# Ten weight slots of a 32-expert MoE stage, joined into one ring in the order of consumption

## The reference, cut to what matters

```
logits = hf @ w_router + b_router                    # 256 tokens, 32 experts
top_val, top_idx = lax.top_k(logits, 4)
gates = softmax(top_val)
for each expert e, on the tokens that chose it:
    gu = xb @ w_gate_up[e] + b_gate_up[e]            # (1024 x 2048): 8 MB
    gate = min(gu[:, :1024], 7);  up = clip(gu[:, 1024:], -7, 7)
    glu = gate * sigmoid(1.702 * gate)
    y = ((up + 1) * glu) @ w_down[e] + b_down[e]     # (1024 x 1024): 4 MB
    out[tokens] += gate_weight * y
x = x + gate2 * out;  return rms_norm(x, final_norm_g)
```

## Time and profile before

| | us |
|---|---|
| median of 3 runs | 1252.24 (1250.06 to 1254.26) |
| profiled execution | 1254.92 |
| its span, first to last instruction | 1253.1 |
| TensorE busy | 1140.6 (91%) |
| VectorE busy | 451.5 (36%) |
| data moved | 465.13 MB, mean 371 GB/s |
| instructions | 13746 |

### The profile page before, as it was taken

One profiled execution on the slowest core, in us unless ns is written; L12 is line 12 of the kernel. 1 busy time (PEld: TensorE's weight loads), 2 busy tenths in 40 slices (PEclk: granted clock), 3 DMA queues, 4 the chain that ended last, 5 costly groups with the idle time before them and its releaser, 6 DMA issues.

```text
span 1253.1 us, 13746 instructions
## 1 busy us (share of the span) xinstructions
PE 1140.6 (91%) x5333; PEld 521.6 (42%) x5333; DVE 451.5 (36%) x975; ACT 116.4 (9%) x217; POOL 11.8 (1%) x12
## 2 busy tenths in 40 slices
PE   3999999997999999999999999998989898999996
PEld 1588678864333333333232323232333333232322
DVE  3467236527613141432313141313233231313143
ACT  1111122611000000000000000000000000000000
POOL 0000000003000000000000000000000000000000
PEclk9999999998999999999999999999999999999999
DMA  9997941167659999999999999999999999999994
GB/s 341 366 370 303 391 163 68 67 248 292 269 212 429 428 427 429 428 429 428 428 428 429 429 427 428 427 430 429 427 428 427 430 429 427 428 427 430 428 428 190
DMA packets 49025, 465.13 MB, mean 371 GB/s; under 512 B 5466, under 2 KB 6220, under 8 KB 21100
## 3 DMA queue, kind: packets, MB, share of 16 engines
q1 hardware_dynamic: 45592, 461.11, 88.3%
q10 hardware_dynamic: 3412, 3.74, 1.0%
HBM read 463.79 MB, written 1.05 MB: 371 GB/s over the span
## 4 chain that ended last, share of the span: by engine, by line
PE 52%; DMA 40%; DVE 4%; SPq 2%; issue 1%; ACT 1%; DVEq 0%; ACTq 0%
DMA arena<-in_w_gate_up 40%; PE ps L806 12%; PE ps L824 11%; PE ps L566 8%; PE ps L833 5%; PE ps L689 2%; PE ps L712 2%; PE ps L661 2%; PE ps L788 1%; SPq L370 1%; PE ps L560 1%; PE ps L483 1%; PE ps L529 1%; PE ps L796 1%; PE ps L516 1%
## 5 line engine op out<-in xcount | busy, mean ns | idle before, releaser
L806 PE MATMUL ps<-arena 128*64 128x512 f32 x2048 | 455.2, 597 | 33.9 <-DMA arena<-in_w_gate_up 33.9
L806 PEld LDWEIGHTS ps<-arena 128*64 128x64 f32 x2048 | 141.4, 137 | 345.9 <-issue 273.2
L824 PE MATMUL ps<-arena 128*64 128x512 f32 x1024 | 226.0, 594 | 0.7 <-issue 0.7
L1431 DVE TENSOR_SCALAR arena<-ps 128x512 f32<-128x512 f32 x32 | 22.1, 691 | 380.2 <-PE ps L806 380.2
L824 PEld LDWEIGHTS ps<-arena 128*64 128x64 f32 x1024 | 72.1, 137 | 149.3 <-issue 146.0
L1470 DVE TENSOR_TENSOR arena<-ps,arena 64x512 f32<-64x512 f32 x64 | 44.1, 689 | 188.5 <-PE ps L824 188.1
L566 PE MATMUL ps<-arena 128*128 128x256 f32 x448 | 97.7, 380 | 0.0
L566 PEld LDWEIGHTS ps<-arena 128*128 128x128 f32 x448 | 85.1, 190 | 13.8 <-issue 2.6
L1070 ACT ACTIVATE arena<-arena 128x512 f32<-128x512 f32 x32 | 20.1, 630 | 607.3 <-DVE arena L1431 607.3
L788 PE MATMUL ps<-arena 128*128 128x128 f32 x512 | 63.1, 283 | 10.8 <-DVE arena L1485 10.8
L788 PEld LDWEIGHTS ps<-arena 128*128 128x128 f32 x512 | 60.1, 197 | 14.7 <-issue 14.7
(11 more groups left out here) (240 smaller groups left out, 629.5 us busy)
## 6 DMA issues: line engine op xcount, KB each, us to landing
arena<-in_w_gate_up SPq DMA_DIRECT2D x128, 2048.0 KB, 31.3
arena<-in_w_down SPq DMA_DIRECT2D x62, 2048.0 KB, 23.6
arena<-in_w_ada SPq DMA_DIRECT2D x12, 2048.0 KB, 17.1
arena<-in_w_in SPq DMA_DIRECT2D x10, 2048.0 KB, 16.5
arena<-in_w_mix_out SPq DMA_DIRECT2D x2, 2048.0 KB, 8.9
arena<-in_w_down SPq DMA_DIRECT2D x4, 1024.0 KB, 28.5
arena<-in_w_hy_out SPq DMA_DIRECT2D x1, 2048.0 KB, 15.0
arena<-in_w_attn_out SPq DMA_DIRECT2D x1, 2048.0 KB, 19.0
```

The lines of the kernel that those rows point to most:

```text
L806: last = mm(ps[64 * h:64 * h + 64, 4 + b, :], hTp[:, k, s * 64:(s + 1) * 64], w[:, o:o + 512], start=False, stop=(k == KD - 1))
L824: last = mm(ps[64 * h:64 * h + 64, 6, :], lhs, rows[c][:, qq * D + h * 512:qq * D + (h + 1) * 512], start=(q == 0), stop=(q == 7))
```

## The change

The ten areas become one list `slots`. Weight blocks are numbered in the order in which TensorE consumes them (`block_at`: ten of pair 0, then twelve to each pair), block n goes to slot n mod 10, and waits until block n-10 is consumed, with a single counter `consumed` that both gate_up and down count up. Since twelve blocks to a pair don't divide by ten, the slot of each block differs from pair to pair; pairs 1 to 14 are written out with constants on the SyncE and TensorE queues (`FIXED` = 15), and the loop begins at pair 15, with slots fixed as `last_slot`. The first fill goes in the ring's order, and the slot `dft` is filled between the first two of the front's areas.

```
-        gu_a = ring[:NJ]
-        gu_b = [span("dft", 0, 4096), span("ur", 4096, 4096), span("ur", 0, 4096), span("x", 0, 4096)]
-        dn_row = ring[NJ:NJ + NC]
-        last_row = [at("ring", 2048 * c, 2048) for c in range(4)]
+        in8, in9, hy, att, mix0, mix1 = (ring[where[b] % 6] for b in blocks[-6:])
+        slots = [in8, span("dft", 0, 4096), in9, hy, att, span("ur", 4096, 4096), mix0, mix1,
+                 span("ur", 0, 4096), span("x", 0, 4096)]
+        NS = len(slots)
+        A0, DB, B0, DA, PAIR = 0, NJ, NJ + NC, 2 * NJ + NC, 2 * (NJ + NC)
+        FIXED = E // 2 - 1
+        def block_at(p, i):
+            return PAIR * (p - 1) + NS + i if p else i
+        def place(p, i):
+            if isinstance(p, int):
+                n = block_at(p, i)
+                return slots[n % NS], s_slot[n % NS], 16 * (n // NS + 1)
+            k = last_slot[i]
+            per = last_slot.count(k)
+            before = last_slot[:i].count(k)
+            return slots[k], s_slot[k], p * (16 * per) + 16 * (uses_before[k] + before + 1 - FIXED * per)
+        def used(p, i):
+            return block_at(p, i) if isinstance(p, int) else p * PAIR + (NS - PAIR + i)
...
+            wait_used(blocks[-6])
+            gate_up(place(0, 0), 0, 0)
+            sp.wait_ge(S["s_ps"], 2 * HEADS)
+            gate_up(place(0, 1), 0, 1)
+            wait_used(blocks[-5])
+            gate_up(place(0, 2), 0, 2)
+            wait_used(blocks[-4])
+            gate_up(place(0, 3), 0, 3)
+            gate_up(place(0, 4), 1, 0)
+            sp.wait_ge(S["pj_sb"], KD)
+            gate_up(place(0, 5), 1, 1)
+            sp.dma_start(b_down[0:E, :], a["b_down"][0]).then_inc(S["bd_in"], 16)
+            wait_used(blocks[-2])
+            gate_up(place(0, 6), 1, 2)
+            wait_used(blocks[-1])
+            gate_up(place(0, 7), 1, 3)
             sp.wait_ge(S["mix_ps"], 4)
-            gate_up(gu_b[2], s_gub[2], 1, 2)
+            down(place(0, 8), 0, 0)
             sp.wait_ge(S["res_ps"], 1)
             sp.wait_ge(S["xs_rdy"], TT)
             sp.wait_ge(S["bc_sb"], 8)
-            gate_up(gu_b[3], s_gub[3], 1, 3)
+            down(place(0, 9), 0, 1)
 
             def pair_of(p, e_a, e_prev, e_b):
                 for j in range(NJ):
-                    sp.wait_ge(S["gu_used"], p * 8 + (j - 7))
-                    gate_up(gu_a[j], s_gua[j], e_a, j)
+                    sp.wait_ge(S["consumed"], used(p, A0 + j - NS + 1))
+                    gate_up(place(p, A0 + j), e_a, j)
                 for c in range(NC):
-                    sp.wait_ge(S["dn_used"], p * 4 + (c - 3))
-                    down(c, e_prev)
+                    sp.wait_ge(S["consumed"], used(p, DB + c - NS + 1) if isinstance(p, int) else used(p, DA + c - PAIR + 1))
+                    down(place(p, DB + c), e_prev, c)
                 for j in range(NJ):
-                    sp.wait_ge(S["gu_used"], p * 8 + (j - 3))
-                    gate_up(gu_b[j], s_gub[j], e_b, j)
+                    sp.wait_ge(S["consumed"], used(p, B0 + j - NS + 1))
+                    gate_up(place(p, B0 + j), e_b, j)
                 for c in range(NC):
-                    sp.wait_ge(S["dn_used"], p * 4 + (c - 1))
-                    down(c, e_a)
+                    sp.wait_ge(S["consumed"], used(p, DA + c - NS + 1) if isinstance(p, int) else used(p, DB + c + 1))
+                    down(place(p, DA + c), e_a, c)
...
-            pair_of(1, 2, 1, 3)
+            for p in range(1, FIXED):
+                pair_of(p, 2 * p, 2 * p - 1, 2 * p + 1)
             sp.wait_ge(S["tables"], 2)
-            with sp.Fori(2, n_pairs) as p:
+            with sp.Fori(FIXED, n_pairs) as p:
...
-            with pe.Fori(1, n_pairs) as p:
+            for p in range(1, FIXED):
+                pair_of(p)
+            pe.wait_ge(S["tables"], 2)
+            n_pairs = pe.value_load(table_i[0:1, 48:49], min_val=E // 2, max_val=ITEMS // 2)
+            with pe.Fori(FIXED, n_pairs) as p:
+                pair_of(p)
```

More of the change, by code:

```diff
@@ L142, in build @@
         NJ, NC = 4, 2
-        gu_a = ring[:NJ]
-        gu_b = [span("dft", 0, 4096), span("ur", 4096, 4096), span("ur", 0, 4096), span("x", 0, 4096)]
-        dn_row = ring[NJ:NJ + NC]
-        last_row = [at("ring", 2048 * c, 2048) for c in range(4)]
-        fgB = at("ring", 4096 * 2, D)
-        junk = at("ring", 4096 * 3, 2048)
         y = b_down = span("prm", 0, D)
@@ L265, in build @@
             x1T_dve x1T_act part_ps part_sb log_ps top_rdy top_exp m_rdy rank_ps cnt_ps cnt_sb ex_ps g_all gt_ps gt_sb tables h2_rdy
-            gu_used dn_used tr_done sc_done ga_done pt_done
+            consumed tr_done sc_done ga_done pt_done
             g_rdy sig_rdy act_rdy actT_rdy y_rdy ga_sb pt_sb sel_rdy wt_rdy mask_rdy
@@ L270, in build @@
         s_front = [sem(f"front_in{j}") for j in range(6)]
-        s_gua = [sem(f"gate_up_a_in{j}") for j in range(NJ)]
-        s_gub = [sem(f"gate_up_b_in{j}") for j in range(NJ)]
-        s_dn = [sem(f"down_in{c}") for c in range(NC)]
+        s_slot = [sem(f"slot_in{k}") for k in range(10)]
+        s_last = [sem(f"last_down_in{c}") for c in range(4)]
         pj_bank = (0, 1, 4, 5)
@@ L327, in build @@
         w_gu, w_dn = a["w_gate_up"], a["w_down"]
+        in8, in9, hy, att, mix0, mix1 = (ring[where[b] % 6] for b in blocks[-6:])
[6 more added lines that the diff above has]
+            return PAIR * (p - 1) + NS + i if p else i
+        last_slot = [block_at(FIXED, i) % NS for i in range(DA)] + [block_at(FIXED, DB + c) % NS for c in range(NC)]
+        uses_before = [sum(n % NS == k for n in range(block_at(FIXED, 0))) for k in range(NS)]
+        def place(p, i):
[8 more added lines that the diff above has]
+            return block_at(p, i) if isinstance(p, int) else p * PAIR + (NS - PAIR + i)
+        final_slot = [block_at(FIXED + 1, c) % NS for c in range(NC)]
+        last_row = [slots[final_slot[c // 2]][:, 2048 * (c % 2):2048 * (c % 2 + 1)] for c in range(4)]
+        fgB = slots[last_slot[0]][:, 0:D]
+        junk = slots[last_slot[1]][:, 0:2048]
         block = ctx.enter_context(nc.Block())
@@ L364, in _, with gate_up @@
                     sp.dma_start(dft, a["t_dft"].rearrange("(t p) f -> p t f", p=P)).then_inc(S["dft_in"], 16)
-            def gate_up(dst, landed, expert, j):
+            def gate_up(place_, expert, j):
+                dst, landed, _ = place_
                 src = w_gu[expert, j] if isinstance(expert, int) else w_gu[bass.ds(expert, 1), j]\
@@ L370, in gate_up, with down @@
                 sp.dma_start(dst, src).then_inc(landed, 16)
-            def down(c, expert):
+            def down(place_, expert, c):
+                dst, landed, _ = place_
                 src = w_dn[expert, c] if isinstance(expert, int) else w_dn[bass.ds(expert, 1), c]\
                     .rearrange("o p n -> p (o n)")
[L375 to L390, removed]
+                sp.dma_start(dst, src).then_inc(landed, 16)
+            wait_used(blocks[-6])
[14 more added lines that the diff above has]
+            gate_up(place(0, 7), 1, 3)
             sp.wait_ge(S["mix_ps"], 4)
-            gate_up(gu_b[2], s_gub[2], 1, 2)
+            down(place(0, 8), 0, 0)
             sp.wait_ge(S["res_ps"], 1)
@@ L422, in _ @@
             e_b = expert_of(q * 2 + 1)
-            sp.wait_ge(S["gu_used"], q * 8 + 4)
+            sp.wait_ge(S["consumed"], used(q, A0 + NJ))
             for c in range(4):
                 sp.dma_start(last_row[c], w_dn[bass.ds(e_b, 1), c // 2, :, 2048 * (c % 2):2048 * (c % 2 + 1)]
-                             .rearrange("o p n -> p (o n)")).then_inc(s_gua[c], 16)
+                             .rearrange("o p n -> p (o n)")).then_inc(s_last[c], 16)
             sp.dma_start(fgB, a["final_norm_g"][:].partition_broadcast(P)).then_inc(S["fg_in"], 16)
@@ L797, in gate_up @@
                            sel_bias[E * b:E * b + E, h * 512:(h + 1) * 512], start=True, stop=False)
+                first = (B0 if s else A0) if not isinstance(p, int) or p else NJ * s
                 for j in range(NJ):
-                    w, landed = (gu_b[j], s_gub[j]) if s else (gu_a[j], s_gua[j])
-                    pe.wait_ge(landed, p * 16 + 16)
+                    w, landed, count = place(p, first + j)
+                    pe.wait_ge(landed, count)
                     for kk in range(2):
@@ L807, in gate_up @@
                                           w[:, o:o + 512], start=False, stop=(k == KD - 1))
-                    last.then_inc(S["gu_used"], 1)
+                    last.then_inc(S["consumed"], 1)
             def act_transpose():
@@ L813, in act_transpose, with down @@
                 last.then_inc(S["tr_done"], 1)
[L815 to L819, removed]
+            def down(pieces):
+                n = KD // len(pieces)
+                for c, (rows, landed, count) in enumerate(pieces):
+                    pe.wait_ge(landed, count)
                     for qq in range(n):
@@ L824, in down @@
```

(42 more changed lines are left out.)

## The result

| | before | changed |
|---|---|---|
| median, us | 1252.01 (1250.06 to 1254.26, 4 runs) | 1243.28 (1242.55 to 1244.15, 4 runs) |
| ratio to before | | 0.993 (0.9911 to 0.9949) |
| profiled execution, us | 1254.92 | 1242.55 |
| its span, us | 1253.1 | 1240.7 |

The change made the kernel 8.7 us faster (0.7%); 10.8 were forecast. Between the two profiled spans lie 12.4 us, 3.7 more than between the medians.

A forecast was written before the change was run, and what follows sets the result against it. Weight transfers were taken as the bound (58.75 us a pair, TensorE 55.0). An earlier block 14 (-13.8 us) and code fetches (+3.0) sum to -10.8 us: profiled 1244.1, median 1241.4, range 1237 to 1251.

The forecast's parts named there:

- The bound and the place: Transfers bound the kernel once stocked blocks are used; the one costly standstill is 345 to 359 us, before pair 1's first down.
- Part 1: Block waits in the ring: block 14 leaves at 344.9 instead of 358.67, gaining 13.8 us at every later landing.
- gap at block 20: Pair 1's tight place, margin about 1 us: no gap taken; a missed one would cost at most about 2.9 us.
- Part 2: The first fill of ten blocks in a new order, dft's moved to near 220 us: cost and gain 0.
- Part 3: TensorE's code written out for fourteen pairs: 28 more code packets beside the full weight queue, costing 3 us.
- near the even end: Choice of 3 us for code fetches, between 1.9 us spread evenly over 16 engines and 31 us on one.
- The 1.1 us over the first four fetches: Block 14's issue to pair 15's B3 landing: 854.8 us due, 855.9 taken; the four fetches within it cost 1.1 us together.
- Part 4: SyncE, VectorE and the end: SyncE's code under 0.1 us each way, work behind the last gate_up landing unchanged at 38.5 us.
- One engine for all code: Rival: all code fetches pass one transfer engine, costing 31 us against 13.8 gained, so +17, 1269 us; chance 8%.
- The fetches cost as in the first pair: Rival: 28 fetches at 0.55 us each cost 15 us, giving 1254; at half, 7.7 us, giving 1246; chance 12%.
- Free: Rival: code fetches cost the transfers nothing, the full 13.8 us stays, 1238.4 us; chance 15%.
- The idle time comes back: Rival: gaps before block 20 or several, 2.9 us each: 1244.3 us with one, 1247 with two; chance 10%.

The follow-up runs named there:

- e2: The changed kernel with one more SyncE wait ahead of block 14, until nine of the first ten blocks are consumed: 1256.63 us, ratio 1.0033 to the kernel before.
- e3: The changed kernel with FIXED = 2, only pair 1 in the ring, fixed slots and a six-block wait from pair 2: 1248.56 us, ratio 0.9969 to before.
- e6: The changed kernel with FIXED = 3, pairs 1 and 2 in the ring, the loop from pair 3: 1246.27 us, ratio 0.9956 to before.
- e9: The changed kernel with the first fill's dft transfer put back some 40 us later: 1243.32 us, ratio 0.9933 to before.
- e1: The kernel before, slots and waits kept, with pairs 1 to 14 written out on TensorE and SyncE: 1257.77 us, ratio 1.0043 to before.
- e8: The kernel before with pairs 1 to 14 written out on SyncE alone, TensorE keeping its loop: 1252.15 us, ratio 1.0004 to before.
- e5: The changed kernel with FIXED = 5, pairs 1 to 4 written out in the ring, the loop from pair 5: 1241.01 us, ratio 0.9907 to before.

## Why the prediction was right, point by point

**The bound and the place.** Right. Removing one stretch of idle transfers moved every later landing; putting back the wait in it (e2) took the gain away.

**Part 1.** Right in size: 13.8 us forecast, 12.9 to 13.4 us came back in e2. No gap at block 20, as forecast, with the interval of 28.8 us computed to 0.1. One sentence there was too short. It said that running up to ten blocks ahead "brings nothing". In the steady state that is so, but early on it is what keeps the 13.8 us, as e3 and e6 show for pairs 2 and 3. The calculation had assumed the ring there; it hadn't said that its depth does the work.

**Part 2.** Right: 0, by e9.

**Part 3.** The mis-sized term. The number of packets was right (42, forecast 41), and so was the kind of cost: an addition to the transfers and not a stall of TensorE. The size was 3 us and measured 4.8, in e1 5.7 on the medians. The step that was off is "near the even end": I spread the hits over 16 engines, and they fell on 8. An even spread over 8 of the packet's 1.1 us gives 29 x 1.1 / 8 = 4.0. Each hit cost its engine 1.5 us, though, and not the 1.1 for which the packet is seen; 29 x 1.5 / 8 = 5.4 us is what the spread of the landings grew by. What the further 0.4 us of each hit are wasn't isolated. The 1.1 us over the first four fetches, 0.28 a packet, was set aside as too dear a sample; 0.17 a packet came in the end, and the 3 us taken stood for 0.11.

**Part 4.** Right: behind the start on the last gate_up block come 38.5 us in both profiles (1253.1 - 1214.61 and 1240.7 - 1202.25), and SyncE's code alone cost nothing (e8).

**The rivals.** One engine for all code would have given 1269, and fell by measurement. The rule of lowest-numbered engines in the Trainium skill (DMA: Bandwidth & Descriptors, Why a DMA increments its semaphore by 16 and not by 1) speaks of DMAs that a kernel issues and doesn't carry over to code fetches: the landings show eight engines hit. "The fetches cost as in the first pair" priced them at 7.7 to 15 us, where 4.8 were measured. "Free" fell with e1. "The idle time comes back" didn't happen in the changed kernel, but e3 shows the same mechanism with a shorter ring.

**What would show it.** The last landing was forecast near 1204 and came at 1202.2, with the profile's early front in it; without those 3.7 us it would have been 1205.9. That the profiled execution (1242.55) lies even below its forecast of 1244.1 is luck of the same kind. The first wait for weights was forecast in pair 7 or 8, from 733 on, and came in pair 7 at 729, earlier by about as much. Pairs longer than 58.9 us were named as the sign of dear fetches, and two pairs in four show it.

## What to carry to other kernels

Where two resources are close in pace, find which is slower in which part of the run. A lead of the transfers has to be stored in buffers for as long as the consumer is the slower side; after that a shallower wait does as well. Here the ten-block ring was kept for pairs 1 to 4 in e5, with the loop from pair 5. That was the smallest version run that has the whole gain (1241.01 us with 22 code packets, ratio 0.9907), with a median 2.2 us below the changed kernel's in the same rounds, though the intervals overlap.

Code that is written out wasn't free in this kernel, which is bound by its transfers: it went over the same engines as the data, and what counted was the engine that landed last. And a transfer moved into idle time gained nothing, because the buffers would have been full in time anyway.

## What the runs showed of the hardware

TensorE's code came in packets of 16 KB, one for about each half pair, and by the landings through eight of the sixteen transfer engines in rotation. Each held one part of the weight stream back by about 1.5 us, where the packet itself is seen for 1.0 to 1.1 us. With 42 instead of 13 such packets the time from block 14's issue to the last gate_up landing grew by 4.8 us; the page's slices show 425 to 429 GB/s in that time, where they showed 427 to 430 before. TensorE's own pair didn't get longer for it (54.94 us against 55.01). A loop of TensorE that was fetched once, with 2 packets, brought no further packet over the following pairs (13 in the whole run, the last at 397.6 us).
